# Copies of v from ScalarE to VectorE, and modulation quads one pair later, in a two-layer GLA and attention kernel

## The chip, the cores and the metric

One core of a Trainium2 chip runs the whole kernel. The metric is the device time of one execution in microseconds (us). TensorE does the matmuls, VectorE (DVE in the rows) and ScalarE (ACT) the elementwise work, GpSimd (POOL) one elementwise job, and SyncE (SP) issues most of the transfers from the memory.

## The reference

Two layers work on 256 latent tokens and 256 context tokens of width 2048, all in fp32. Layer 0 is a bidirectional gated linear attention (GLA) with four heads, layer 1 a differential softmax attention with eight heads.

```
for i in range(2):
    shift, scale, gate = split(silu(c) @ ada_w[i] + ada_b[i], 3)      # "modulation", and the same for c_ctx
    h  = rmsnorm(x, norm_w[i]) * (1 + scale) + shift                  # 256 x 2048; hc from ctx alike
    p  = h @ w_in                                                     # q, k, v, g
    layer 0, per head: q, k 256 wide, v 512 wide
        la = log_sigmoid((h @ a1) @ a2 + gate_b) / 16                 # forward and backward
        o  = chunked GLA of q, k, v with the decays exp(cumsum(la)), both directions, context first
    layer 1, per head: softmax(q1 k1) v - lam * softmax(q2 k2) v over latent and context tokens
    y  = (rmsnorm(o) * silu(g)) @ w_out
    x  = x + gate * y                                                 # ctx alike in layer 0
```

## The kernel before

**Projections.** All 512 tokens stand as four tiles of 128. A projection is cut into chunks of 512 output columns, and a chunk c into 8 pairs of weight tiles (`PAIRS`, two of 128 rows each). Each weight and each activation is split into a high part and a remainder, and three matmuls (`ops` in `project`, line 722) make up one fp32 product: 24 matmuls for a pair with four token tiles. The four token tiles accumulate in PSUM banks 0 to 3 (line 722 `bank[t]`). A bank is given back with the semaphore `freed[t]`, for which TensorE waits at the first pair of the next chunk (line 715). So whoever copies a chunk out of the banks decides when TensorE may begin the next one.

**The weights' way.** SyncE loads pair p into one of four slots (`RING`) of `raw`. ScalarE makes the high part (`split`, line 440) as soon as TensorE has finished the pair four before, GpSimd the remainder (line 425), and when GpSimd is done SyncE loads the pair four further on (`load_pair`). `load_chunk` is SyncE's list: at pair x it waits for GpSimd's split of x.

**A GLA head.** Head h owns three chunks: c = 3h (q and k), c+1 (v), c+2 (the gate g). Between c and c+1 TensorE makes the gate logits (`gate_logits`, line 785). From them VectorE and ScalarE make four sets of decayed q and k ("units" 0 to 3): VectorE's `unit_tildes(h, n)` subtracts, ScalarE's `decays(h, n)` exponentiates, VectorE multiplies and signals `til_ok`. TensorE's `unit_scores(h, n)` (lines 789 and after) turns them into scores. There is one set of buffers, so `unit_tildes(h, n)` for n > 0 first waits for `unit_done`, the scores of unit n - 1. In the kernel before, unit 0 is scored behind pair 5 of chunk c+1, units 1, 2, 3 behind pairs 0, 3, 6 of chunk c+2, and `head_outputs` (line 840) follows chunk c+2. ScalarE copies v out of the four banks (line 544) between its splits of pairs 2 and 3 of chunk c+2. Each engine does its list in the order in which it is written.

**Modulation in the background.** The modulation of layer 1 and the gates of layer 0 are made in 16 batches beside the projections. A batch i is four quads m = 4i to 4i + 3; a quad is one transfer of 1 MB of `ada_w` and four small matmuls (line 683; x8 in the trace, which lists two passes of each). `quad_after(m)` names the pair behind which TensorE does quad m, and the sum of the batch (`modulation_sum`, line 691) stands one pair behind its last quad. Each GLA head has an even batch (positions 0, 1, 3, 5 of the head's 24 pairs) and an odd one. There are two buffers for the transfers, so SyncE issues the block of quad m (`background_quad`, line 309) behind the loads of the pair that is 4 behind `quad_after(m - 2)`, the last use of the same buffer. Bank 7 holds the sum, and in its upper half scores of units 0 and 1; `unit_scores(h, 0)` waits until VectorE has taken the odd batch (`take_modulation`).

Of the kernel before, what the change touches and what calls it, by code (L numbers as in the profile page):

```python
# [31 lines left out]
ACT = mybir.ActivationFunctionType  # L32
# [5 lines left out]
NT = 4  # L38
# [4 lines left out]
PAIRS = NK // 2  # L43
RING = 4
# [21 lines left out]
def quad_after(m):  # L66


    i, q = m // 4, m % 4
    if i < 2 * G_HEADS:  # L70
        return 3 * (i // 2) * PAIRS + ((7, 8, 10, 11) if i % 2 else (0, 1, 3, 5))[q]
    if i < 2 * G_HEADS + 4:
        return (OUT0 + i - 2 * G_HEADS) * PAIRS + (0, 1, 3, 5)[q]
    return (DIFF + 4 * (i - 2 * G_HEADS - 4)) * PAIRS + (5, 7, PAIRS + 2, PAIRS + 5)[q]
# [21 lines left out]
def build(nc, io, out):  # L96
    with ExitStack() as ctx:
# [3 lines left out]
        def sem(name):  # L101
            return ctx.enter_context(nc.semaphore(name))
# [33 lines left out]
        def view(at, *shape):  # L136
            n = int(np.prod(shape))
            v = work[:, at:at + n]
            if len(shape) == 1:
                return v  # L140
            names = "abcd"[:len(shape)]
            kw = {names[i]: shape[i] for i in range(1, len(shape))}
            return v.rearrange(f"p ({' '.join(names)}) -> p {' '.join(names)}", **kw)
# [13 lines left out]
        v_sb = view(2048, NT, CW)  # L157
# [38 lines left out]
        bank = [ctx.enter_context(nc.psum_tensor(f"bank{i}", [P, CW], F32)) for i in range(8)]  # L196
# [18 lines left out]
        pair_done = sem("pair_done")  # L215
        acc_ok = sem("acc_ok")
        freed = [sem(f"freed{i}") for i in range(NT)]
# [49 lines left out]
        def _(sp):  # L267
# [79 lines left out]
            def load_chunk(c, parts, following):  # L347


                for p in range(PAIRS):  # L350
                    if p < RING:
                        load_pair(c, p + RING, parts)
                    elif following is not None:
                        load_pair(c + 1, p - RING, following)
                    for m in range(4 * BACKGROUND):
                        if c * PAIRS + p == (quad_after(m - 2) + 4 if m >= 2 else 0):
                            background_quad(m)

            wg = io["gla_w_in"][0].rearrange("(k p) n -> p k n", p=P)
# [70 lines left out]
        def _(act):  # L430
            st = Steps(act, act_step)

            def log_and_exp():
                act.preload_act_table_set("natural_log_exp_and_others")
# [7 lines left out]
            def splits(c, ps):  # L442
                for p in ps:
                    split(c, p)
# [33 lines left out]
            def modulation_rows(a):  # L478


                b = bank[6 + a % 2] if a < STARTUP else bank[7]
                act.wait_ge(ada_used, 4 * a + 4)
                if a > 0:
                    act.wait_ge(mod_sum, a)
                act.activation(ada_rows[:], b[:], ACT.Copy).then_inc(row_ok, 1)
# [30 lines left out]
            def gla_head(h, first):  # L516
                c = h * 3
                if not first:
                    splits(c, range(4, 8))
                splits(c + 1, range(0, 2))  # L520
                modulation_rows(STARTUP + 2 * h)
                splits(c + 1, range(2, 4))

                for n in range(4):
                    act.wait_ge(logit_out, h * 4 + (n + 1))
                    st.step(act.activation(ln_t[:, n], bcum[:, n], ACT.Abs))
                    st.wait()
                    st.step(act.activation(ln_t[:, n], ln_t[:, n], ACT.Exp, scale=-1.0))
                    st.wait()
                    act.activation(ln_t[:, n], ln_t[:, n], ACT.Ln, bias=1.0).then_inc(ln_ok, 1)  # L530

                splits(c + 1, range(4, 5))
                decays(h, 0)
                splits(c + 1, range(5, 8))
                modulation_rows(STARTUP + 2 * h + 1)
                splits(c + 2, range(0, 2))
                decays(h, 1)
                splits(c + 2, range(2, 3))
                for t in range(NT):
                    if t == NT - 1:  # L540
                        act.wait_ge(pair_done, c * PAIRS + (2 * PAIRS + RING))
                    else:
                        act.wait_ge(acc_ok, h * 9 + (3 + t + 1))
                    act.activation(v_sb[:, t], bank[t][:], ACT.Copy).then_inc(freed[t], 1)
                splits(c + 2, range(3, 5))
                decays(h, 2)
                splits(c + 2, range(5, 8))
                decays(h, 3)
                splits(c + 3, range(0, 4))
                for t in range(NT):  # L550
                    if t == NT - 1:
                        act.wait_ge(pair_done, c * PAIRS + (3 * PAIRS + RING))
                    else:
                        act.wait_ge(acc_ok, c * 3 + (6 + t + 1))
                    act.activation(silu_g[:, t], bank[t][:], ACT.Silu).then_inc(freed[t], 1)
                log_and_exp()

                for t in range(NT):
                    act.wait_ge(o_out, h * 4 + (t + 1))
                    if t > 0:  # L560
                        act.wait_ge(sq_ok, h * NT + (NT + t))
                    act.activation(o_sq, o_sb[:, t], ACT.Square, accum_out=stat[:, 0, t:t + 1])\
                        .then_inc(sq_ok, 1)
                rsqrt(h + 2, NT)

            gla_head(0, True)
            for h in range(1, G_HEADS):
                gla_head(h, False)
# [105 lines left out]
        def _(pe):  # L674
# [121 lines left out]
            def unit_scores(h, n):  # L796

                pe.wait_ge(til_ok, h * 4 + (n + 1))  # L800
                if n == 0:
                    pe.wait_ge(ada_taken, STARTUP + 2 * h + 2)
                back, first = n < 2, n == 0
                score(bank[4][:, 0:256], tok(kb, C0), qB if back else qA, first)
                score(bank[5][:, 0:256], tok(kb, C1), qA if back else qB, first)
                if back:
                    score(bank[6][:, 256:384], tok(kb, X1), tok(qh, X0), first)
                    score(bank[5][:, 256:384], tok(kb, C1), tok(qh, C0))
                else:
                    score(bank[6][:, 128:256], tok(kb, X0), tok(qh, X1))  # L810
                    score(bank[4][:, 384:512], tok(kb, C0), tok(qh, C1))
                for t in range(NT):
                    b, at_ = DIAG[t]
                    low, high = slice(0, HALF), slice(HALF, P)
                    if back:
                        score(bank[b][high, at_:at_ + HALF], k1[:, t], q1[:, t])
                        col = 256 + t * HALF
                        score(bank[7][low, col:col + HALF], tok(k2, t, HALF), tok(q2, t, HALF))
                        last = score(bank[7][high, col:col + HALF], tok(k2, t, HALF, HALF), tok(q2, t, HALF, HALF))
                    else:  # L820
                        score(bank[b][low, at_ + HALF:at_ + P], k1[:, t], q1[:, t])
                        score(bank[b][low, at_:at_ + HALF], tok(k2, t, HALF), tok(q2, t, HALF))
                        last = score(bank[b][high, at_ + HALF:at_ + P], tok(k2, t, HALF, HALF),
                                     tok(q2, t, HALF, HALF))
                last.then_inc(unit_done, 1)
# [18 lines left out]
            def gla_head(h, before=None, gates=None):  # L844
                c = h * 3
                if h > 0:
                    pe.wait_ge(d2_ok, h)
                project(c, lambda t: c, False, before=before)
                if gates is not None:
                    gates()  # L850
                gate_logits(h)
                project(c + 1, lambda t: c + 1, True,
                        after=lambda p: unit_scores(h, 0) if p == 5 else None)

                def after(p):
                    if p in (0, 3, 6):
                        unit_scores(h, {0: 1, 3: 2, 6: 3}[p])

                project(c + 2, lambda t: c + 2, True, after=after)
                head_outputs(h)  # L860
# [94 lines left out]
        def _(dve):  # L955
            st = Steps(dve, dve_step)

            def complete(n, c, t, tiles=NT):

                if t == tiles - 1:  # L960
                    dve.wait_ge(pair_done, c * PAIRS + (PAIRS + RING))
                else:
                    dve.wait_ge(acc_ok, n + (t + 1))
# [147 lines left out]
            def gla_head(h, first):  # L1111
                c = h * 3
# [31 lines left out]
                take_modulation(STARTUP + 2 * h + 1, 3, h * 4)  # L1144
                unit_tildes(h, 1)

                unit_tildes(h, 2)

                d2 = bank[7][:, 256:512].rearrange("p (t s) -> p t s", s=HALF)
# [268 lines left out]
```

## Time and profile before

| what | value |
|---|---|
| median of 3 runs | 1868.02 us (1867.91 to 1872.02) |
| the profiled execution, its own time | 1867.91 us |
| its span in the profile | 1865.8 us |
| mean granted clock of TensorE | 0.96 of full |
| TensorE busy | 1724.9 us, 92% of the span, 7996 matmuls |
| VectorE busy | 828.2 us, 44% |
| ScalarE busy | 551.1 us, 30% |
| GpSimd busy | 717.3 us, 38% |
| read from memory | 262.14 MB, 142 GB/s over the span |

Times in the rows are us from the span's start. The busy share is an average over the stages, and a matmul's end is modelled, since matmuls overlap: 24 matmuls of 0.39 us each take 5.5 to 5.7 us. A stretch of the trace shows better than the shares whether TensorE waits there.

### The profile page before, as it was taken

How to read it: one execution, taken by the hardware profiler on the slowest of the kernel's cores; microseconds unless marked ns; L12 is line 12 of the kernel's file. 1: busy time of each engine (PE TensorE's matmuls, PEld its weight loads, DVE VectorE, ACT ScalarE, POOL GpSimd, SP SyncE). 2: the span in 40 equal slices, each digit the busy share in tenths (PEclk: the TensorE clock that was granted, in tenths of full speed). 3: DMA queues.
4: the chain of work that ended last, by engine and by line, in shares of the span. 5: the costliest groups of instructions: out<-in, count | busy, mean ns of one | idle time of the engine just before them, and what ended most of it. 6: DMA issues, size and time to landing. Idle time of an engine off the chain costs nothing.

```text
span 1865.8 us, 19637 instructions
## 1 busy us (share of the span) xinstructions
PE 1724.9 (92%) x7996; PEld 1282.4 (69%) x7996; DVE 828.2 (44%) x1235; ACT 551.1 (30%) x805; POOL 717.3 (38%) x297
## 2 busy tenths in 40 slices
PE   3869999999999999979999799999999999997698
PEld 0237787778668777847677577877777787776476
DVE  0125543244154315455111358374673847557641
ACT  1122333332333323323222323232332323233142
POOL 0023333333333333313333227364563536545176
PEclk9579999999999999999999899999999999999799
DMA  8975422542343254214555327233533623433054
GB/s 317 387 258 166 146 91 79 172 147 92 125 166 107 68 178 160 86 50 141 182 167 186 114 65 234 79 125 125 169 115 108 194 80 125 135 113 124 12 173 131
DMA packets 185581, 265.53 MB, mean 142 GB/s; under 512 B 16090, under 2 KB 99988, under 8 KB 184980
## 3 DMA queue, kind: packets, MB, share of 16 engines
q1 hardware_dynamic: 180660, 256.68, 42.0%
q10 hardware_dynamic: 4832, 7.60, 1.3%
q8 instruction: 63, 1.03, 0.2%
q14 instruction: 26, 0.21, 0.0%
HBM read 262.14 MB, written 2.10 MB: 142 GB/s over the span
## 4 chain that ended last, share of the span: by engine, by line
PE 79%; DVE 12%; DMA 5%; SPq 2%; ACT 1%; issue 1%; POOL 0%; ACTq 0%; DVEq 0%
PE bank L722 63%; PE bank L683 4%; DMA w_raw<-in_ada_w 4%; PE bank L840 2%; PE bank L789 2%; PE bank L927 2%; PE bank L911 2%; DVE acts_lo L1057 1%; DVE work L1241 1%; DVE work L1264 1%; DVE u L1218 1%; SPq L317 1%; PE bank L737 1%; PE bank L785 1%; DVE work L1283 1%; PE bank L691 1%
## 5 line engine op out<-in xcount | busy, mean ns | idle before, releaser
L425 POOL TENSOR_TENSOR w_lo<-w_raw,w_hi 128x1024 fp32r<-128x1024 f32 x288 | 715.0, 2492 | 1134.8 <-ACT w_hi L440 1134.6
L722 PE MATMUL bank<-w_lo,acts_hi 128*128 128x512 f32 x1664 | 671.9, 404 | 30.0 <-DVE work L1296 10.6
L722 PE MATMUL bank<-w_hi,acts_hi 128*128 128x512 f32 x1664 | 654.1, 393 | 0.0
L722 PE MATMUL bank<-w_hi,acts_lo 128*128 128x512 f32 x1664 | 654.0, 393 | 0.0
L440 ACT ACTIVATE w_hi<-w_raw 128x1024 fp32r<-128x1024 f32 x288 | 302.9, 1057 | 875.5 <-PE bank L722 811.3
L722 PEld LDWEIGHTS bank<-w_lo,acts_hi 128*128 128x128 f32 x1664 | 315.6, 190 | 144.5 <-issue 50.8
L722 PEld LDWEIGHTS bank<-w_hi,acts_lo 128*128 128x128 f32 x1664 | 315.7, 190 | 68.4
L722 PEld LDWEIGHTS bank<-w_hi,acts_hi 128*128 128x128 f32 x1664 | 316.0, 190 | 63.0 <-issue 1.7
L1013 DVE TENSOR_TENSOR mod<-bank,cols 128x8 f32<-128x8 f32 x24 | 3.9, 164 | 380.7 <-PE bank L691 380.7
L683 PE MATMUL bank<-ada_w,silu_p 128*32 128x512 f32 x640 | 98.2, 690 | 27.6 <-DMA ada_w<-in_ada_w 27.6
L722 PE MATMUL bank<-acts_hi,w_lo 128*128 128x512 f32 x256 | 104.4, 408 | 11.5 <-DVE acts_lo L1057 11.5
L722 PE MATMUL bank<-acts_lo,w_hi 128*128 128x512 f32 x256 | 100.6, 393 | 0.0
L722 PE MATMUL bank<-acts_hi,w_hi 128*128 128x512 f32 x256 | 100.4, 392 | 0.0
L1057 DVE TENSOR_TENSOR acts_lo<-work,acts_hi 128x512 fp32r<-128x512 f32 (+1 forms) x64 | 69.7, 1089 | 28.3 <-ACT acts_hi L467 27.8
L722 PEld LDWEIGHTS bank<-acts_hi,w_lo 128*128 128x128 f32 x256 | 48.6, 190 | 33.1 <-DVE acts_lo L1057 12.1
L1087 DVE TENSOR_TENSOR work<-work 128x512 f32<-128x512 f32 x16 | 23.5, 1468 | 83.0 <-PE bank L789 82.9
L467 ACT ACTIVATE acts_hi<-work 128x512 fp32r<-128x512 f32 (+1 forms) x64 | 35.4, 572 | 76.0 <-DVE work L1049 46.8
L1241 DVE TENSOR_TENSOR work<-work 128x256 f32<-128x256 f32 (+1 forms) x40 | 55.9, 1439 | 0.0
L722 PEld LDWEIGHTS bank<-acts_lo,w_hi 128*128 128x128 f32 x256 | 48.5, 189 | 10.6
L722 PEld LDWEIGHTS bank<-acts_hi,w_hi 128*128 128x128 f32 x256 | 48.7, 190 | 10.1 <-issue 0.7
L683 PEld LDWEIGHTS bank<-ada_w,silu_p 128*32 128x32 f32 x640 | 13.3, 113 | 60.5 <-DMA ada_w<-in_ada_w 36.2
L1336 DVE COPY work<-bank 128x512 f32<-128x512 f32 x16 | 10.3, 686 | 89.9 <-PE bank L920 89.9
(148 smaller groups left out, 1423.7 us busy)
## 6 DMA issues: line engine op xcount, KB each, us to landing
ada_w<-in_ada_w SPq DMA_DIRECT2D x80, 1024.0 KB, 7.7
w_raw<-in_diff_w_in SPq DMA_DIRECT2D x256, 256.0 KB, 2.9
w_raw<-in_gla_w_in SPq DMA_DIRECT2D x192, 256.0 KB, 3.0
w_raw<-in_ada_w SPq DMA_DIRECT2D x16, 1024.0 KB, 9.6
w_raw<-in_gla_w_out SPq DMA_DIRECT2D x64, 256.0 KB, 3.4
w_raw<-in_diff_w_out SPq DMA_DIRECT2D x64, 256.0 KB, 3.4
u<-in_x SPq DMA_DIRECT2D x2, 1024.0 KB, 13.9
u<-in_ctx SPq DMA_DIRECT2D x2, 1024.0 KB, 16.5
```

What stands on the lines that cost most here:

```text
L425: pool.tensor_tensor(w_lo[:, p % RING], raw[:, p % RING], w_hi[:, p % RING].bitcast(F32), ALU.subtract).then_inc(w_split, 1)
L440: act.activation(w_hi[:, p % RING], raw[:, p % RING], ACT.Copy).then_inc(w_hi_ok, 1)
L467: act.activation(hi[:, k, 0:n * P], src[:, k % 2, 0:n * P], ACT.Copy).then_inc(hi_ok, 1)
L683: last = pe.matmul(b[32 * j:32 * j + 32, :], silu_p[:, 4 * q + j, :], quad_slot[slot][:, j, :], start=(q == 0), stop=(q == 3), skip_group_ ...
L722: last = pe.matmul(bank[t][:], a, b, start=(k == 0 and i == 0), stop=(k == NK - 1 and i == 2))
L789: return pe.matmul(out_, k_part, q_part, start=start, stop=True, skip_group_check=True)
L840: last = pe.matmul(bank[4 + t % 3][:], at[:, b, col:col + P], v_sb[:, kt, :], start=(i == 0), stop=(i == len(READ[t]) - 1))
L911: pe.matmul(bank[4 + i][:], qT[:, m, t * P:(t + 1) * P], kT[:, m, :], start=True, stop=True)\
L927: last = pe.matmul(bank[6][:, t * A_DV:(t + 1) * A_DV], aT[:, kt, t * P:(t + 1) * P], kv[:, kt, A_DV:CW], start=(kt == 0), stop=(kt == NT ...
L1057: dve.tensor_tensor(lo[:, k, 0:width], buf[:, k % 2, 0:width], hi[:, k, 0:width].bitcast(F32), ALU.subtract).then_inc(acts_ok, 1)
L1087: dve.tensor_tensor(tokens(q2, HALF), b64, b64[:, :, mid:mid + 1].broadcast_to([P, 8, HALF]), ALU.subtract)
L1241: last = dve.tensor_tensor(g(dst)[:, :, :, a], g(src)[:, :, :, 1 - a], g(tab)[:, :, :, a], ALU.mult)
```

## The change

Five edits, all in the GLA heads or in the schedule of the quads. The copies of v move from ScalarE to VectorE, behind `unit_tildes(h, 1)`. ScalarE's list around them changes: the split of pair 0 of chunk c+2 now stands before the odd batch's row copy. Unit 0 is scored behind pair 6 instead of pair 5 of chunk c+1. The odd batch's quads stand behind positions 8, 9, 11, 12 of the head instead of 7, 8, 10, 11. All background blocks are issued 5 instead of 4 pairs behind the last use of their buffer.

```diff
@@ quad_after
     if i < 2 * G_HEADS:
-        return 3 * (i // 2) * PAIRS + ((7, 8, 10, 11) if i % 2 else (0, 1, 3, 5))[q]
+        return (3 * (i // 2) + i % 2) * PAIRS + ((0, 1, 3, 4) if i % 2 else (0, 1, 3, 5))[q]
@@ load_chunk (SyncE)
-                        if c * PAIRS + p == (quad_after(m - 2) + 4 if m >= 2 else 0):
+                        if c * PAIRS + p == (quad_after(m - 2) + 5 if m >= 2 else 0):
                             background_quad(m)
@@ gla_head (ScalarE)
                 splits(c + 1, range(5, 8))
+                splits(c + 2, range(0, 1))
                 modulation_rows(STARTUP + 2 * h + 1)
-                splits(c + 2, range(0, 2))
+                splits(c + 2, range(1, 2))
                 decays(h, 1)
-                splits(c + 2, range(2, 3))
-                for t in range(NT):
-                    if t == NT - 1:
-                        act.wait_ge(pair_done, c * PAIRS + (2 * PAIRS + RING))
-                    else:
-                        act.wait_ge(acc_ok, h * 9 + (3 + t + 1))
-                    act.activation(v_sb[:, t], bank[t][:], ACT.Copy).then_inc(freed[t], 1)
-                splits(c + 2, range(3, 5))
+                splits(c + 2, range(2, 5))
                 decays(h, 2)
@@ gla_head (TensorE)
                 project(c + 1, lambda t: c + 1, True,
-                        after=lambda p: unit_scores(h, 0) if p == 5 else None)
+                        after=lambda p: unit_scores(h, 0) if p == 6 else None)
@@ gla_head (VectorE)
                 take_modulation(STARTUP + 2 * h + 1, 3, h * 4)
                 unit_tildes(h, 1)
+                for t in range(NT):
+                    complete(h * 9 + 3, c + 1, t)
+                    dve.tensor_copy(v_sb[:, t], bank[t][:]).then_inc(freed[t], 1)
                 unit_tildes(h, 2)
```

## Rows read from the trace of the kernel before

**Rows 1.** The page, its chain that ended last, by engine.
```profile
PE 79%; DVE 12%; DMA 5%; SPq 2%; ACT 1%; issue 1%; POOL 0%; ACTq 0%; DVEq 0%
```
**Rows 2.** Windows: length; busy PE, PEld, DVE, ACT, POOL; TensorE's granted clock; DMA share, GB/s.
```profile
317.00:484.00 167.00, 167.00 (x821) 125.92 (x818) 63.54 (x109) 55.33 (x87) 58.70 (x24) 1.00 0.39 127
```
**Rows 3.** TensorE's waits, 830 us to the end (total, times, longest).
```profile
PE bank L683 <- DMA ada_w<-in_ada_w: 1.7, 1, 1.7
...
PE bank L722 <- POOL w_lo L425: 0.9, 3, 0.4
```
**Rows 4.** Chain in time, TensorE, head 1 (start, duration, what, count).
```profile
334.94 1.00 PE bank L683 x8
...
361.10 3.63 PE bank L785 x8
...
383.49 5.67 PE bank L722 x24
...
404.61 16.54 PE bank L722 x72
...
527.74 3.63 PE bank L785 x8
```
**Rows 5.** Timeline of ScalarE, head 1: the copies of v.
```profile
413.71 2.64 ACT L544 ACTIVATE work<-bank 128x512 f32<-128x512 f32 x4 [2.16 <-PE bank L722]
```
**Rows 6.** VectorE's groups: the like copy of k (busy us, mean ns).
```profile
L1119 DVE COPY work<-bank 128x512 f32<-128x512 f32 x8 | 5.5, 692 | 0.0
```
**Rows 7.** Timeline of VectorE, head 1: tildes 0, then tildes 1.
```profile
375.60 0.69 DVE L1087 TENSOR_TENSOR work<-work 128x512 f32<-128x512 f32 x1
...
380.54 0.69 DVE L1094 TENSOR_TENSOR work<-work 128x512 f32<-128x512 f32 x1 [2.97 <-ACT work L514]
...
384.56 2.88 DVE L1097 TENSOR_TENSOR work<-work 128x512 f32<-128x512 f32 x1
...
388.47 0.35 DVE L1107 TENSOR_SCALAR work<-work,g_tot 128x256 f32<-128x256 f32 x1
...
404.64 1.73 DVE L1087 TENSOR_TENSOR work<-work 128x512 f32<-128x512 f32 x1 [7.82 <-PE bank L789]
...
414.65 0.68 DVE L1097 TENSOR_TENSOR work<-work 128x512 f32<-128x512 f32 x1
...
416.37 0.35 DVE L1107 TENSOR_SCALAR work<-work,g_tot 128x256 f32<-128x256 f32 x1
```
**Rows 8.** Timeline of GpSimd, head 1: splits beside tildes 0 and 1.
```profile
381.54 5.35 POOL L425 TENSOR_TENSOR w_lo<-w_raw,w_hi 128x1024 fp32r<-128x1024 f32 x2 [7.20 <-ACT w_hi L440]
...
411.62 2.56 POOL L425 TENSOR_TENSOR w_lo<-w_raw,w_hi 128x1024 fp32r<-128x1024 f32 x1 [5.79 <-ACT w_hi L440]
```
**Rows 9.** Timeline of SyncE, head 1: issues with pairs 5, 13, 14.
```profile
327.33 0.43 SPq L309 DMA_DIRECT2D ada_w<-in_ada_w  x1
...
384.11 3.60 SPq L329 DMA_DIRECT2D w_raw<-in_gla_w_in  x4
387.75 0.43 SPq L309 DMA_DIRECT2D ada_w<-in_ada_w  x1
```
**Rows 10.** The tile `ada_w`: its transfers, from issue to landing.
```profile
DMA to landing us min/median/max: 5.3/7.7/10.5
```
**Rows 11.** Timeline of TensorE at the second output chunk of layer 0.
```profile
895.85 0.80 PE L722 MATMUL bank<-w_lo,acts_hi 128*128 128x512 f32 x1 [2.35 <-DVE work L1215]
```
**Rows 12.** Windows of 1 us there, columns as in rows 2.
```profile
895.00:896.00 1.00, 0.15 (x1) 0.15 (x1) 0.97 (x3) 0.00 (x0) 0.00 (x0) 0.79 0.17 63
...
899.00:900.00 1.00, 1.00 (x6) 0.82 (x5) 0.00 (x0) 0.91 (x3) 0.00 (x0) 1.00 0.74 209
```
**Rows 13.** Chain in time behind three gaps of TensorE.
```profile
895.85 5.18 PE bank L722 x15
...
1003.88 5.29 PE bank L722 x15
...
1070.46 8.53 PE bank L722 x24
```

## Prediction

> **What bounds the kernel now.** I read the page first, for its chain that ended last: TensorE is 79% of it [rows 1]. Then the windows by head: in 167 us cut out of the GLA heads (layer 0) TensorE is busy for 167.00 us, at the full granted clock [rows 2]. So in the part that the change touches TensorE waits for nobody. Whatever leaves ScalarE there gives back nothing; each wait given to TensorE is paid in full, and nothing later can absorb it, since the next head is again without a gap. What could be won outside the heads is in the waits of TensorE after 830 us: 1.7 us for an `ada_w` block and 0.9 us for GpSimd's splits [rows 3], 2.6 us together, 0.14%.
>
> The pace of head 1 is in TensorE's chain [rows 4]: its gate logits begin at 361.10, those of head 2 at 527.74, so a head takes 166.64 us. A weight pair of 24 matmuls takes 5.67 us, 5.51 us in a run of three (16.54/3), a quad 1.0 us. I write p0 to p7 for the pairs of a chunk and U for the end of unit 0's scores (404.61 in rows 4). Behind it stand p6, p7 and p0 of chunk c+2 with no gap, because ScalarE empties the four banks at 413.71 to 416.35 [rows 5], just as each bank's last matmul ends: p7 ends at 404.61 + 11.02 = 415.63, and the first bank had been free for over a microsecond.
>
> **The v copies.** They leave ScalarE (4 in 2.64 us, hidden) and go to VectorE, at 0.69 us each [rows 6], behind `unit_tildes(h, 1)`. That function waits for unit 0's scores, and those move one pair later, from behind p5 to behind p6. So only p7 (5.51 us) now stands between U and the first matmul of chunk c+2, which waits for bank 0. What VectorE has to do from U to the first free bank: in head 1 of before tildes 1 runs from 404.64 to 416.72, 12.1 us [rows 7], with ScalarE's exponentials inside. Its two long products take 2.88 us where GpSimd works beside them and 0.68 us where it doesn't; GpSimd's rows show one split at that time (411.62 to 414.18), and two back to back beside tildes 0 (381.54 to 386.89) [rows 8]. After the change the splits of pairs 2 and 3 of chunk c+2 are both ready when `decays(h, 1)` ends: ScalarE has no more copies between them, and p6 and p7 have ended by U + 5.5. That is the picture of tildes 0: 375.60 to 388.82, 13.2 us [rows 7]. I take 13.2; 12.1 is the low end. The Trainium skill (SBUF — State Buffer, "Who interferes with whom") says that a VectorE instruction with two SBUF inputs contends with a GpSimd one that reads SBUF, and that one blocks for the whole instruction. By that rule two splits mean two long products, as the 2.88 and 0.68 us here bear out; with proportional sharing it would be some 12.1 us.
>
> First bank free at U + 13.2 + 0.7 = U + 13.9; TensorE is there at U + 5.5. **Stall 8.4 us per head** (7.3 us with 12.1). The other three copies, 0.6 to 0.7 us apart, stay ahead of three matmuls of a bank (0.69 us). Behind TensorE's wait hang p0 of c+2, unit 1, ScalarE's split of pair 4 and all the rest of the head; behind VectorE's copies only tildes 2, which waits for unit 1 anyway. Nothing is won back.
>
> **The quads.** Their count and cost (1.0 us each) stay. In odd batches they move from behind pairs 7, 8, 10, 11 of the head to 8, 9, 11, 12: the gate logits and all of VectorE's and ScalarE's work up to the splits of pair 13 come 1.0 us earlier, chunk c+1 is 1.0 us longer, sum zero. The modulation sum moves with them from behind pair 12 to behind 13; ScalarE's row copy (0.6 us) has 5.5 us for it. The orders: `+ 5` issues a block one pair later. SP comes to pair x when GpSimd has split x, that is some 3.6 us behind TensorE's end of pair x - 4. So a block whose predecessor in its buffer was used two positions back has now, where the distance in `quad_after` is 3, only two pairs of cover. These are:
>
> - third quad of each odd batch, position 11. It is issued with pair 8 + 5 = 13. SP's row for that pair in head 1 is 384.11 [rows 9], late because ScalarE does the splits of pair 13 only after `decays(h, 0)`. Two weight issues stand before it (0.84 us), and all of it is 1.0 us earlier: 383.96. Landing takes 7.7 us in the median of all blocks, 5.3 to 10.5 at the ends [rows 10], so 391.7. TensorE is through pair 11 at 383.49 + 5.67 - 1.0 = 388.2 [rows 4]. **Stall 3.6 us per head**; with 5.3 us it is 1.1, with 10.5 us 6.3. The next block, position 12, is ordered with pair 14 at 387.75 [rows 9], lands at 395.5, with 10.5 us at 398.3, and is wanted at 391.7 + 1.0 + 5.7 = 398.4: hidden.
> - third quad of each even batch, position 3, and its like in layer 0's output chunks, eight in all. Issued with pair 5: 327.33 in head 1 [rows 9], landed at 335.0; wanted when TensorE ends pair 3 at 334.94 [rows 4]. On the edge, and taken at nothing: the pairs 2 and 3 hide it, with nothing to spare, and a landing of 10.5 us would cost 2.9 us.
>
> Elsewhere the distance is four pairs or more. SP waits for no quad longer than before, and the weight loads stand one block less deep in the queue, where TensorE doesn't wait for them.
>
> **The clock.** The trace shows what a gap does. At 895.85 TensorE resumes after 2.35 us of waiting for a bank [rows 11]; its clock is below full in that window and back at 1.00 in the one from 899 [rows 12], and 15 matmuls take 5.18 us [rows 13] where 15 x 0.23 = 3.45 are due: 1.7 us lost. The boundary of the last two output chunks (1003.88) shows 5.29 for the same 15 [rows 13], and it is so at the one between them. After the long gap at 1061 to 1070 us, 24 matmuls take 8.53 us instead of 5.51, 3.0 lost [rows 13]. Neither length is the stall's; a gap that leaves TensorE cold at all costs at least what the short one did, and the row for 2.35 us is nearest to 3.6. I take 1.7 us for each stall, between 0 (no fall) and 3.0 (both, the longer recovery). The Trainium skill (TensorE: Matmul & The Clock Gate, Part 1) puts the penalty of the ramp below 1% of a typical kernel's span; that would be under 19 us here, and eight falls of 1.7 us stay under it.
>
> **Sum.** Per head 3.6 + 1.7 + 8.4 + 1.7 = 15.4 us, four heads 61.6 us. On the profiled execution (1867.91 us, span 1865.8, 0.1 us from the median of the three runs): 1929.5 us, +3.3%.
>
> **Rivals.**
>
> *The transfer comes in time.* If the third odd block lands within 4.2 us of its order, or SP reaches pair 13 over 3 us earlier, only the bank stall is left: 4 x (8.4 + 1.7) = 40.4 us, 1908 us. Against it: no landing under 5.3 us in the trace. For it: chains of three engines set SP's moment, and one block did land in 5.3.
>
> *The clock holds.* Both stalls without a fall: 4 x 12.0 = 48 us, 1916 us. Against it: three falls out of three at 2.35 us.
>
> *More blocks late.* The eight on the edge late by 1.0 us and half of them with a fall: + 8 + 7 = 1944 us. For it: they have no slack; against: in head 1 the sum above has the block there within 0.1 us of its use.
>
> *Not slower.* The stall at chunk c+2 vanishes if the 13.9 us from U to the free bank fit into pair 7. It decides at 5.5 us; ScalarE's exponentials and the four short subtractions before them alone take 4.9 us (375.60 to 380.54). The third block would have to be in time too. Then 1865.3 to 1868 us, the lower by the 2.6 us above. I see nothing for it but that the order of waits might be misread.
>
> **Numbers.** Forecast 72%, transfer in time 12%, clock holds 6%, more late 7%, not slower 3% (half of it faster). Range 1906 to 1944: it takes in the first three cases and, up to its own time, the fourth. The likeliest case's own range is 1915 (short chain and landing in 5.3 us: 4 x 3.6 = 14.4 less) to 1944 (the longer recovery in both stalls, 4 x 2.6 = 10.4 more, and landings 1 us later, 4 more). A measurement of this kernel tells about 0.3% (5.6 us) from no change. Faster 1.5%, same 1.5%, slower 97%.
>
> **What the profile after would show.** TensorE's waits get a group for its L722 matmuls released by VectorE's copy of v, four times, about 8.4 us each, and one for L683 released by the DMA of `ada_w`, four of 3 to 4 us; VectorE's chain from unit 0 to the first copy is 13.9 us with both long products at 2.88; the clock falls eight times in the heads, and 24 matmuls there take some 7.2 us instead of 5.5; a head lasts 182 us. Wrong I am if p0 of chunk c+2 follows p7 without a gap, if the block of position 11 lands before pair 11 ends, or if the gaps are there and the clock stays at 1.00.

## The result and the profile after

The changed kernel takes 1943.86 us in the median of 4 runs (1935.37 to 1948.86), the kernel before 1868.86 us (4 runs, 1867.91 to 1872.02). The ratio is 1.0394, with a 95% interval of 1.0355 to 1.0433: 75 us or 3.9% slower. The forecast was 1929.5 us, the range 1906 to 1944. The profiled execution took 1944.98 us, its span is 1942.9 us, 77.1 us more than before. The numbers of lines have moved by 6: 722 is now 716, 683 is 677, 785 is 779, 789 is 783.

TensorE's waits over the whole span, largest first (total, times, longest). The second row is new; before there was no wait of that kind.

```profile
PE bank L677 <- DMA ada_w<-in_ada_w: 42.2, 19, 13.9
PE bank L716 <- DVE work L1143: 33.0, 4, 8.2
```

L1143 is VectorE's copy of v. Four waits of 8.2 us, one in each head: the stall that was forecast at 8.4. The first row holds the start of the kernel too (27.6 us of such waits before). In the heads alone it is this, from 180 to 900 us; before, TensorE had no such wait there:

```profile
PE bank L716 <- DVE work L1143: 33.0, 4, 8.2
PE bank L677 <- DMA ada_w<-in_ada_w: 11.6, 6, 4.0
```

In the odd batches of the four heads the late blocks cost 0.9 (two waits), 2.6, 3.7 and 4.0 us. The sixth wait, 0.4 us, is for a block of head 2's even batch.

The chain in order of time in head 1, from the gate logits to those of head 2, answers to [rows 4] (start, duration, what, count):

```profile
375.85 3.64 PE bank L779 x8
...
399.71 6.75 DMA ada_w<-in_ada_w
406.47 0.04 issue
406.51 1.09 PE bank L677 x8
407.60 7.20 PE bank L716 x24
...
427.86 2.40 PE bank L783 x32
430.26 0.02 issue
430.28 0.69 DVE work L1081
...
436.51 2.75 DVE work L1090
439.26 2.75 DVE work L1091
...
443.05 0.35 DVE work L1101
443.40 0.61 DVE work L1143
444.01 0.14 issue
444.14 7.69 PE bank L716 x24
...
557.93 3.64 PE bank L779 x8
```

Before, this chain held nothing but TensorE. Now it goes through the transfer of a quad's block, and through the whole of tildes 1 from U = 430.26. Logits to logits are 182.08 us, 166.64 before. Both long products take 2.75 us each in the chain (2.83 with their tail), 2.88 and 0.68 before in tildes 1 [rows 7]. And 24 matmuls take 7.20 us behind the first gap and 7.69 behind the second, where 5.5 to 5.7 are due. GpSimd's two splits stand back to back beside the products, as they did beside tildes 0 [rows 8]; its timeline:

```profile
436.22 5.24 POOL L425 TENSOR_TENSOR w_lo<-w_raw,w_hi 128x1024 fp32r<-128x1024 f32 x2 [11.11 <-ACT w_hi L440]
```

TensorE's timeline gives the two gaps their lengths (in brackets), and windows of 1 us at the second give the clock (eighth number):

```profile
406.51 1.09 PE L677 MATMUL bank<-ada_w,silu_p 128*32 128x512 f32 x8 [2.56 <-DMA ada_w<-in_ada_w]
...
444.14 0.77 PE L716 MATMUL bank<-w_lo,acts_hi 128*128 128x512 f32 x1 [8.24 <-DVE work L1143]
```

```profile
442.00:443.00 1.00, 0.00 (x0) 0.00 (x0) 1.00 (x5) 0.00 (x0) 0.00 (x0) 0.50 0.41 59
...
446.00:447.00 1.00, 1.00 (x4) 0.81 (x3) 0.00 (x0) 0.00 (x0) 0.00 (x0) 0.50 0.00 0
...
449.00:450.00 1.00, 1.00 (x6) 0.83 (x5) 0.00 (x0) 0.00 (x0) 0.00 (x0) 1.00 0.00 0
```

The clock had already fallen to half (1.2 of 2.4 GHz) while TensorE waited, and it is back in full some 5 us after the work has begun again.

### The profile page after: what moved, and what is told of

Same layout as the page of the kernel before. It is cut to its first block, busy times and chain, and to the rows that moved or that the text cites. A ratio compares the mean times of both kernels' runs of the same rounds, so it can differ in the third digit from the quotient of the medians.

```text
span 1942.9 us, 19637 instructions
## 1 busy us (share of the span) xinstructions
PE 1753.1 (90%) x7996; PEld 1298.3 (67%) x7996; DVE 836.0 (43%) x1251; ACT 541.9 (28%) x789; POOL 715.0 (37%) x297
## 4 chain that ended last, share of the span: by engine, by line
PE 68%; DVE 17%; DMA 7%; ACT 2%; SPq 2%; POOL 1%; issue 1%; ACTq 0%; DVEq 0%
PE bank L716 54%; DMA w_raw<-in_ada_w 4%; PE bank L677 3%; DMA ada_w<-in_ada_w 3%; PE bank L834 2%; PE bank L783 2%; PE bank L921 2%; POOL w_lo L425 1%; PE bank L905 1%; DVE work L1261 1%; DVE acts_lo L1051 1%; DVE work L1134 1%; DVE work L1238 1%; DVE u L1215 1%; SPq L317 1%
## 5 line engine op out<-in xcount | busy, mean ns | idle before, releaser
L716 PE MATMUL bank<-w_lo,acts_hi 128*128 128x512 f32 x1664 | 682.4, 410 | 65.6 <-DVE work L1143 33.0
L716 PE MATMUL bank<-w_hi,acts_hi 128*128 128x512 f32 x1664 | 661.0, 397 | 0.0
L716 PEld LDWEIGHTS bank<-w_lo,acts_hi 128*128 128x128 f32 x1664 | 320.6, 193 | 189.5 <-issue 89.0
L716 PEld LDWEIGHTS bank<-w_hi,acts_lo 128*128 128x128 f32 x1664 | 320.0, 192 | 70.4
L716 PEld LDWEIGHTS bank<-w_hi,acts_hi 128*128 128x128 f32 x1664 | 321.6, 193 | 64.4 <-issue 1.7
L716 PEld LDWEIGHTS bank<-acts_hi,w_lo 128*128 128x128 f32 x256 | 48.5, 189 | 31.8 <-issue 11.6
L1081 DVE TENSOR_TENSOR work<-work 128x512 f32<-128x512 f32 x16 | 19.3, 1209 | 90.3 <-PE bank L783 90.1
```

Of the source, the lines that this page charges most:

```text
L716: last = pe.matmul(bank[t][:], a, b, start=(k == 0 and i == 0), stop=(k == NK - 1 and i == 2))
```

## The experiments

To tell the causes apart, one edit of the changed kernel is undone, or one edit is made in the kernel before. All times are medians; intervals are those of the ratio to the kernel before, run on the same chip.

| kernel | median us | ratio, 95% interval |
|---|---|---|
| the changed kernel | 1943.86 | 1.0394, 1.0355 to 1.0433 |
| changed, v on ScalarE again (e1) | 1909.23 | 1.0204, 1.0177 to 1.0230 |
| changed, blocks 4 pairs behind again (e2) | 1917.03 | 1.0246, 1.0221 to 1.0272 |
| changed, both undone (e12) | 1879.38 | 1.0055, 1.0037 to 1.0073 |
| before, v on VectorE (e3) | 1879.88 | 1.0048, 1.0032 to 1.0065 |
| before, unit 0 behind pair 6 (e4) | 1884.02 | 1.0077, 1.0050 to 1.0103 |
| before, both (e9) | 1912.96 | 1.0231, 1.0213 to 1.0249 |
| before, blocks 5 pairs behind (e5) | 1896.93 | 1.0144, 1.0117 to 1.0171 |
| changed, wait filled with 38 matmuls (e6) | 1944.62 | 1.0398, 1.0366 to 1.0429 |
| changed, wait filled with 72 matmuls (e10) | 1933.86 | 1.0340, 1.0319 to 1.0361 |
| changed, blocks of layer 1 4 pairs behind (e7) | 1937.95 | 1.0354, 1.0325 to 1.0382 |
| before, banks emptied first, layer 0 (e8) | 1853.37 | 0.9911, 0.9890 to 0.9932 |
| before, the same in layer 1 too (e11) | 1852.36 | 0.9906, 0.9889 to 0.9922 |

### The v copies back on ScalarE

```diff
-                splits(c + 2, range(2, 5))
+                splits(c + 2, range(2, 3))
+                for t in range(NT):
...
+                    act.activation(v_sb[:, t], bank[t][:], ACT.Copy).then_inc(freed[t], 1)
+                splits(c + 2, range(3, 5))
@@ VectorE
-                for t in range(NT):
-                    complete(h * 9 + 3, c + 1, t)
-                    dve.tensor_copy(v_sb[:, t], bank[t][:]).then_inc(freed[t], 1)
```

> The changed kernel with the v copies back on ScalarE (between its splits of pairs 2 and 3 of chunk c+2), all else as changed. Theory (the banks are held by VectorE's order, tildes 1 before the copies): TensorE's four waits of 8.2 us at chunk c+2 go, with their clock falls (some 2.2 us each), 42 us together; ScalarE is then itself a little late, since decays 1 and one split come before its copies: first bank free at U + 6.6 against U + 5.5, 1.1 us per head. 1906 us, 1902 to 1913. Rival (most of the cost sits in the late blocks and the clock, the copies are a side matter): 1925 us or more.

Measured: 1909.23 us, 35 us less than the changed kernel. TensorE's waits in the heads:

```profile
PE bank L684 <- DMA ada_w<-in_ada_w: 15.4, 7, 3.9
...
PE bank L790 <- DVE work L1108: 4.4, 4, 1.1
PE bank L723 <- ACT work L545: 3.4, 4, 0.9
```

The 33.0 us are gone. In their place stand 0.9 us for ScalarE's first copy, as expected, and 1.1 us per head that was not: unit 1 waits for tildes 1, which now end 13.2 us behind U, while p7, the short wait and p0 of chunk c+2 end some 12 us behind it. The late blocks stay, and cost 15.4 us here instead of 11.6: head 0's is 3.8 us late, 0.9 in the changed kernel.

### The order of the blocks back to 4

```diff
-                        if c * PAIRS + p == (quad_after(m - 2) + 5 if m >= 2 else 0):
+                        if c * PAIRS + p == (quad_after(m - 2) + 4 if m >= 2 else 0):
```

> The changed kernel with blocks issued 4 pairs behind the last use of their buffer again, all else as changed. Theory: the third block of each odd batch is issued with pair 12 and lands before its use; TensorE's 11.6 us of waits for ada_w in the heads go with some 6 us of slow clock, and so do 3.3 us of waiting and 2 us of slow clock at the first attention head: 23 us less, 1921 us, 1915 to 1928. Rival (late blocks cost only their wait): 1929 us or more. Rival (the blocks' lateness is absorbed in the waits at chunk c+2): 1940 us and more.

Measured: 1917.03 us, 27 us less. In the heads only the bank waits are left, unchanged:

```profile
PE bank L716 <- DVE work L1143: 33.0, 4, 8.2
```

So neither stall hides in the other.

### One edit at a time in the kernel before

The copies alone:

> The kernel before with one edit: the v copies on VectorE behind tildes 1; unit 0 stays behind pair 5, quads and orders stay. Theory: between U and chunk c+2 stand two pairs, 11.0 us, against a chain of 12.1 + 0.7 us: TensorE waits 1.8 us per head, 7 us, and up to 7 us more if each gap lets the clock fall: 1876 to 1884 us, 1880. Rival (VectorE is the wrong engine for the copies, whatever the order): as much as in the changed kernel, 1905 us or more. Rival (nothing): 1869 us.

Measured: 1879.88 us. The waits in the heads:

```profile
PE bank L716 <- DVE work L1143: 7.0, 4, 1.8
```

1.8 us per head, to the tenth. VectorE is not the wrong engine for these copies, it is merely asked too late. The clock stayed at full behind these four gaps, so the 1880 us, which count some falls there, were met partly by luck: in the profiled run 1.8 us were lost to the clock in layer 0's first output chunk instead, where the kernel before lost none. What makes up the rest was not settled.

Unit 0 alone:

```diff
-                        after=lambda p: unit_scores(h, 0) if p == 5 else None)
+                        after=lambda p: unit_scores(h, 0) if p == 6 else None)
```

> The kernel before with one edit: unit 0 scored behind pair 6 instead of pair 5. ScalarE keeps the v copies. Theory: ScalarE comes to them behind decays 1 and one split, first bank free at U + 6.6 against TensorE's U + 5.5: 1.1 us per head, 4 us; gaps this short leave the clock alone: 1873 us, 1871 to 1880. So the moved unit and the moved copies are small each alone (4 and 7 to 14 us) and 42 us together. Rival (the two add up): their sum is near 42 us.

Measured: 1884.02 us, 11 us over the expectation. Here too there are two waits per head and not one:

```profile
PE bank L789 <- DVE work L1107: 4.4, 4, 1.1
PE bank L722 <- ACT work L544: 3.4, 4, 0.9
```

The wait of unit 1 for tildes 1 had been left out of the sum. From one head's gate logits to the next it is 169.13 us, 2.5 more than before, so the four heads account for 10 of the 14 us over the kernel before; the other 4 are of the size of the spread, and e12, which has the same two waits, lies 9 us over.

Both edits together:

> The kernel before with both edits of e3_v_alone and e4_unit0_alone: the v copies on VectorE behind tildes 1, and unit 0 behind pair 6; quads and orders stay. Theory: one pair (5.5 us) is left between U and chunk c+2 against 13.9 us: TensorE waits 8.2 us per head, the clock falls each time (2.2 us): 42 us more than before, 1912 us, 1908 to 1917; that is far above the sum of the two alone (10 + 14 = 24 us, 1894 us), which is the rival.

Measured: 1912.96 us, 43 us over before, where the two alone are 10 and 14 us over. The wait is that of the changed kernel to the tenth:

```profile
PE bank L716 <- DVE work L1143: 33.0, 4, 8.2
```

This is the core of the change's cost. The bank comes free behind a chain that starts at U. With two pairs of matmuls behind U (11.0 us) the chain is 12.8 us, 1.8 too long; with one pair (5.5 us) both long products are slow, it is 13.7 us, and 8.2 too long.

The order of the blocks alone:

> The kernel before with one edit: blocks issued 5 pairs behind the last use of their buffer. Theory: now the fourth block of each odd batch (position 11, its buffer last used at 8) is issued with pair 13, at 384.96 in head 1, lands at 392.7 and is wanted at 389.2: 3.5 us of waiting per head and some 1.8 us of slow clock, 21 us, and 3.3 us of waiting at the first attention head with up to 2 us of clock: 1893 us, 1885 to 1899. Rival (the lateness comes from the moved quads, not from the order): 1870 us.

Measured: 1896.93 us, 26 us over before. Now TensorE waits in the heads ten times for a block:

```profile
PE bank L683 <- DMA ada_w<-in_ada_w: 14.5, 10, 3.6
```

The moved quads aren't needed for that.

### Both undone

> The changed kernel with the v copies on ScalarE (as in e1_v_on_scalare) and the blocks 4 pairs behind (as in e2_plus4): only the moved unit 0 and the moved quads are left. Theory (the two large costs are separate and the moved quads cost nothing by themselves): as e4_unit0_alone, 1884 us, 1880 to 1889. Rival (the moved quads cost something of their own): 1893 us or more.

Measured: 1879.38 us. With the v copies and the order undone the moved quads and the moved unit are left, and it is no slower than the moved unit alone (the intervals, 1.0037 to 1.0073 and 1.0050 to 1.0103, overlap). The moved quads by themselves cost nothing that can be measured.

### What a gap costs beside its length

The wait at chunk c+2 was filled with matmuls whose result nobody reads (`FILL` is 38, in the second run 72):

```diff
+                for _ in range(FILL):
+                    pe.matmul(bank[7][:, 16:256], hi[:, 0, 0:P], hi[:, 1, 16:256], start=False, stop=True,
+                              skip_group_check=True)
                 project(c + 2, lambda t: c + 2, True, after=after)
```

> The changed kernel with 38 matmuls of no use in each head (240 columns, into columns of bank 7 that nobody reads), placed before TensorE's wait for bank 0 at chunk c+2: they keep TensorE at work for some 7 us of the 8.2 and add nothing to the path. Theory (each of these gaps costs its length and, on top, the clock's fall): the waits fall to some 1 us, the same work as before begins at the same moment, but the 24 matmuls behind take 5.5 us instead of 7.7 to 8.3: 4 x 2.4 = 9.5 us less, 1934 us, 1928 to 1939. Rival (the 24 matmuls are slow for another reason, such as banks that come free one by one): 1944 us.

Measured: 1944.62 us, no gain. The filling was sized wrongly: the 38 matmuls are paced at 0.11 us, not at the 0.19 of a weight load, and take 4.1 us. A gap of 4.1 us is left, and behind it the clock falls all the same: in head 1 the 24 matmuls take 7.33 us (TensorE's timeline):

```profile
443.38 0.47 PE L717 MATMUL bank<-w_lo,acts_hi 128*128 128x512 f32 x1 [4.08 <-DVE work L1147]
```

So this run says nothing on the question; it was put again with 72.

> As e6_filled_wait, with 72 matmuls of no use instead of 38 (these took 4.1 us and left a gap of 4.1 us, in which the clock still fell): now 7.8 of the 8.2 us are filled. Theory: gaps of 0.4 us, no fall, 24 matmuls behind them in 5.6 us instead of 7.7: 4 x 2.2 = 9 us less than the changed kernel, 1935 us, 1929 to 1939. Rival (the slow matmuls have another cause): 1944 us, and the granted clock at the start of chunk c+2 still falls.

Measured: 1933.86 us, 10 us less than the changed kernel. The two intervals still touch (1.0361 and 1.0355), so the gain in time is likely and not shown; the trace is clearer. The chain at the same place as above:

```profile
443.00 0.35 DVE work L1105
443.36 0.61 DVE work L1147
443.97 0.14 issue
444.10 5.71 PE bank L717 x24
```

VectorE's copy ends at the same moment as in the changed kernel (444.0), TensorE goes on at the same moment (444.10, there 444.14), and the same 24 matmuls take 5.71 us instead of 7.69. The granted clock, 0.50 there in the window from 446, is 1.00 here:

```profile
446.00:447.00 1.00, 1.00 (x6) 0.82 (x5) 0.00 (x0) 0.00 (x0) 0.00 (x0) 1.00 0.00 0
```

The banks come free as before, so the 2.0 us are the price of the idle engine's clock.

The other way round, gaps were taken out of the kernel before, where TensorE waits for banks at the boundaries of layer 0's output chunks:

```diff
                         .then_inc(freed[t], 1)
-                    dve.wait_ge(freed[t], c + 1)
+                for t in range(NT):
+                    dve.wait_ge(freed[t], c + 1)
```

> The kernel before with one edit, in layer 0's output chunks: VectorE empties all four banks first and adds the residual behind that, instead of both for each bank in turn. Theory (a gap costs its length plus the clock's fall): the three gaps of TensorE of 2.35 us at the chunks' boundaries go, and with each the 1.8 us that its next 15 matmuls lose: 3 x 4.2 = 12.5 us less, 1857 us, 1854 to 1861. Rival (a gap costs its length alone): 1862 us. Rival (the work only moves to the next wait): 1869 us.

Measured: 1853.37 us, 16 to 17 us less than before (ratio 0.9911). VectorE's timeline at the first boundary shows why: the four products that free the banks come first, the four additions behind them.

```profile
888.92 2.66 DVE L1215 TENSOR_TENSOR work<-bank,work 128x512 f32<-128x512 f32 x4 [3.47 <-PE bank L722]
891.50 4.69 DVE L1219 TENSOR_TENSOR u<-work 128x512 f32<-128x512 f32 x4
```

And TensorE passes the boundary in one run, 11.05 us for 48 matmuls, where before it stood for 2.35 us [rows 11] and then took 5.18 us for 15 [rows 13]:

```profile
885.25 11.05 PE bank L722 x48
```

Three gaps of 2.35 us and three falls of 1.8 us are 12.5 us. The traces show 13.9 us: from one boundary to the next it is 49.4 us here, 53.9 to 54.1 before. The remaining 3 us of the median are open. With the gap's length alone it would be 7 us, which the interval excludes (0.9932 of 1870 us is 13 us less).

> e8_banks_first, and the same reordering in layer 1's output chunks (both banks emptied, then the additions). Theory: of TensorE's 4.9 us of waits for VectorE there some 3 us go, with the fall of the clock behind the longest (1.9 us) where it occurs: 1849 us, 1846 to 1853. Rival (those waits are for the first bank, which doesn't come free earlier): 1853 us, as e8_banks_first.

Measured: 1852.36 us. TensorE's waits for VectorE in layer 1's output chunks fell from 2.7 us in the kernel before to

```profile
PE bank L722 <- DVE work L1366: 0.5, 2, 0.3
```

but the step over e8 (1 us) is less than the runs can tell. It is 0.94% under the kernel before; e8 and e11 are the only versions that beat both kernels.

### The first attention head

```diff
-                        if c * PAIRS + p == (quad_after(m - 2) + 5 if m >= 2 else 0):
+                        if c * PAIRS + p == (quad_after(m - 2) + (4 if m >= 48 else 5) if m >= 2 else 0):
```

> The changed kernel with the blocks of layer 1 (quads 48 and on) issued 4 pairs behind again, the others 5. Theory: TensorE's wait of 5.0 us for ada_w at the first attention head shrinks to 1.7 us, and with it the slow clock behind it where it falls (0 to 2 us): 1944 less 3.3 to 5.3, 1939 us. Rival (that wait is set by something else): 1944 us, the wait stays 5.0.

Measured: 1937.95 us; its interval overlaps that of the changed kernel, so the 6 us are likely but not shown. The wait itself did shrink, from 5.0 to 2.9 us, though not to the 1.7 expected. The kernel before has the shortest such wait of all runs: with the order 4 in layer 1 it is 2.2 to 3.1 us in the other eight, with the order 5 it is 5.0 to 5.5 us in all five. TensorE's waits between 1080 and 1260 us in the changed kernel, and then in this one:

```profile
PE bank L677 <- DMA ada_w<-in_ada_w: 5.0, 1, 5.0
```

```profile
PE bank L677 <- DMA ada_w<-in_ada_w: 2.9, 1, 2.9
```

## Why the prediction was right, and where it was off

**The sign and the mechanism.** Nothing was won on ScalarE, since no wait of TensorE in the heads had been for ScalarE; the waits that the change gave to TensorE were paid in full. The likeliest case named three costs, and all three are in the trace at the places where it put them. The median lies at the upper edge of the range, 14 us over the forecast. That it lies inside, by 0.1 us, is luck: three of the five runs (1944.3, 1944.98 and 1948.86 us) are above 1944, and the edge had been set by other sums than those that came true.

**The bank stall** was forecast at 8.4 us per head and is 8.2 (33.0 in all). Each number in its working held: 13.1 us for tildes 1 (13.2 forecast), both long products slow because GpSimd splits two pairs beside them, 0.6 us for the first copy, one pair of cover. The low end, 12.1 us, belongs to the case with two pairs behind U and appears in e3, where 1.8 us follow from it and 1.8 were measured. The Trainium skill's rule (SBUF — State Buffer, "Who interferes with whom"), that the later of the two instructions blocks for the whole of the other, agrees with the two products of 2.83 us beside GpSimd's two splits of 5.24 us together.

**The late block** was forecast at 3.6 us per head (its own numbers, 391.66 less 388.16, give 3.5) and measured at 0.9, 2.6, 3.7 and 4.0, 11.2 us in place of 14.4. With the block in head 2's even batch it is 11.6. In head 1 it landed 6.75 us after its order instead of 7.7. In head 0 TensorE had itself been slowed before it reached the block (7.7 us for pair 8, most of it at half clock), so that the block was less late, 0.3 us; the other 0.6 us are for the block of position 12, which had been taken as hidden. In e7, where the clock held there, head 0's block was 3.7 us late. e5 shows that the order `+ 5` alone makes such waits.

**The clock** is the term that was sized too small: 1.7 us for each gap, 13.6 us in all. Behind the late blocks of heads 1 to 3 the next 24 matmuls lost 1.7 to 1.9 us, and two quads took 1.9 instead of 1.0; behind the bank stalls they lost 2.2 to 2.8 us. I had taken the price of a 2.35 us gap for one of 8.2 us; the measured ones lie between it and that of the long gap (3.0 us, rows 13). In head 0 it didn't fall behind the block (a gap under 1 us), but during the gate logits, for some 3.4 us. The heads' total by these rows is about 20 us, which makes 33.0 + 11.6 + 20 = 65 us for the four heads against 61.6 forecast; logits to logits it is 182.4, 182.1 and 183.8 us against the 182 forecast. That the clock is the cause, and not the banks that come free one by one, e10 shows. The Trainium skill (TensorE: Matmul & The Clock Gate, Part 1) puts the penalty of the ramp under 1% of a typical kernel's span, 19 us here; the 20 us in the heads just pass it.

**The step that failed** is the sentence "Elsewhere the distance is four pairs or more", from which I took that nothing would be late there. It counts pairs, and pairs aren't equal. In the second chunk of the first attention head a pair has 12 matmuls instead of 24, and SyncE comes late, since ScalarE's and GpSimd's splits are held up by the rotary tables: GpSimd then does three splits in a row. TensorE's wait for the block of that head's position 10 grew from 1.7 us, which had its row before [rows 3], to 5.0. That row said that a block was already late, and an order one pair later had to make it worse. In the two profiled runs that is 3.3 us; by e7 and the other runs the order's own part is some 2 to 3 us. Some 2 us of slow clock stand behind this wait too, but not for the order's sake alone: in e8, with the order 4 and a wait of 2.8 us, 1.7 us are lost there. In time, none of it is shown beyond the spread.

**What is left.** By the starts of like instructions in the two profiled runs, the 77.1 us of span are 65.9 up to the end of the heads, 2.0 in layer 0's first output chunk, 2.6 from the start of layer 1 to a bank wait of 3.3 us at 1306.20 (1235.60 before), 1.4 behind that wait (24 matmuls in 8.44 us, 7.32 before), and 5.1 in layer 1's output chunks. The 2.6 are less than the wait and the clock above, because layer 1's first two pairs lost less to the clock than before (7.10 and 5.78 us for 24 matmuls, 8.53 and 7.31 before). In layer 1's output chunks TensorE's waits for a bank, 2.7 us in all before, grew to 4.9, the longest with a fall of the clock behind it:

```profile
PE bank L716 <- DVE work L1362: 4.9, 5, 2.5
```

The same 4.9 us with 2.5 as the longest stand in the profiled run of e8, whose heads are those of before and which took 1859.63 us against 1851.68 to 1854.17 in its other runs; e7, with heads like the changed kernel's, has 2.6. So this isn't tied to the change; it comes and goes between executions. The 2.0 us are a fall of the clock in layer 0's first output chunk (24 matmuls in 7.36 us), of the same kind. Such falls make up part of the spread of the runs; how much was not settled.

**The rivals.** "The transfer comes in time" (1908 us) is what e2 builds, and it gave 1917; 2 us of that are the clock's higher price, the rest is open, though its profiled run has the 4.8 us of bank waits in layer 1 too. "The clock holds" (1916 us) is refuted in the trace and by e10. "More blocks late" hardly happened: of the eight blocks on the edge one was late, by 0.4 us and with the clock at full (e5 has three such waits, of 0.2 to 0.3 us). "Not slower" had no run for it; its deciding point, 13.9 us to fit into one pair, is what e9 and e3 vary from the other side.

## What to carry to other kernels

A copy that frees a buffer of the bounding engine is best put in front of the work that waits for that engine: the same four copies made TensorE wait not at all (ScalarE, before), 0.9 us (ScalarE, unit 0 later), 1.8 us (VectorE) or 8.2 us (VectorE, unit 0 later) per head, depending on how much work stood between them and their trigger. For layer 0's output chunks e8 shows the gain of that order; VectorE's v copies in front of tildes 1 were not run. Two edits that are each nearly harmless can use up the same slack; look for the slack that both draw on before adding up their prices. And a gap of the matmul engine can be dearer than its length: where the clock fell it was mostly 1.7 to 3 us more, so that many short gaps are worth closing, as emptying the banks first did for 0.9%.

## What was not expected of the hardware

The length of a gap did not settle whether the clock falls. Gaps of 1.8 us (e3, four of four) and two of 0.9 and 1.1 us close together (e4 and e12, four heads each) left it alone, and all gaps of 8.2 us let it fall. In between it went both ways. Behind a gap of 2.2 us in layer 0's first output chunk nothing was lost to the clock in the kernel before and in six experiments, and 1.6 to 1.8 us in the changed kernel and six others. Of the gaps of 2.35 us at the boundaries, three in each of twelve runs, all but three (the first one in e1, e5 and e6) let it fall, at nearly the same price (5.18 to 5.32 us for 15 matmuls in the kernel before). And behind the first gap of 3.3 us in layer 1 it stayed at full in five runs, e8 among them (TensorE's timeline and a window, its granted clock the eighth number):

```profile
1224.57 0.47 PE L722 MATMUL bank<-w_lo,acts_hi 128*128 128x512 f32 x1 [3.27 <-DVE work L1297]
```

```profile
1226.00:1228.00 2.00, 2.00 (x10) 1.64 (x9) 1.93 (x3) 1.97 (x3) 2.00 (x2) 1.00 0.43 123
```

while in the kernel before the clock was at half behind the same gap of 3.27 us, which ends at 1235.60:

```profile
1237.00:1239.00 2.00, 2.00 (x6) 1.53 (x6) 1.93 (x3) 1.97 (x3) 2.00 (x2) 0.50 0.42 135
```

A gap isn't even needed: in head 0 of the changed kernel TensorE stood for only 0.8 us in front of the gate logits, as it did before, and the clock fell during them (0.50 in the windows from 196 to 202). The chain there shows the eight logits' matmuls with 4.90 us, 3.70 before, and 20 matmuls in 6.82 us behind them.

```profile
192.69 0.70 DVE gate_zT L1116
193.39 0.04 issue
193.43 4.90 PE bank L779 x8
198.33 6.82 PE bank L716 x20
```
